# 96 more TensorE instructions ahead of the second recurrence layer's projection: a hybrid RWKV / attention / state-space kernel on one Trainium2 core

## What is computed

```python
for i in range(4):
    kind, j = i % 3, i // 3
    hx = rms_norm(x, norm_g[i]) * (1 + scale_x) + shift_x
    hc = rms_norm(ctx, norm_g[i]) * (1 + scale_c) + shift_c
    if kind == 0:    # h = [hc, hx]
        xs = h + (centred_shift(h) - h) * mu[:, None]        # six mixes
        r, k, v, g = xs[:4] @ w_rkvg
        # decay, iclr from xs[4], xs[5] by low-rank products
        for t in scan order, both directions, per head:       # 16 heads of 64
            sa = state @ kk[t]
            state = state * w[t] - sa (kk[t] * a[t])^T + v[t] k[t]^T
            y[t] = state @ r[t]
        out = (group_norm(y) + bonus) * silu(g) @ w_out
    x = x + gate * out
```

## Time and profile before

| | us |
|---|---|
| median of 3 runs | 7097.44 |
| lowest, highest | 7081.59, 7100.32 |
| profiled execution, its own time | 7083.38 |
| its span | 7081.5 |
| TensorE busy | 5788.8 (82%) |
| VectorE, ScalarE, GpSimd busy | 2986.5, 2066.1, 1883.9 |

### The profile page before, as it was taken

The page is one execution under the profiler, slowest core; times in us unless marked ns, Lnnn a source line. Parts: engine busy times, 40 slices in busy tenths (PEclk is TensorE's granted clock), DMA queues, the critical chain, the costliest instruction groups (busy, mean ns, idle before and its releaser), DMA issues. The chain is left out here.

```text
span 7081.5 us, 214110 instructions
## 1 busy us (share of the span) xinstructions
PE 5788.8 (82%) x92672; PEld 3901.0 (55%) x92672; DVE 2986.5 (42%) x6387; ACT 2066.1 (29%) x3451; POOL 1883.9 (27%) x2006
## 2 busy tenths in 40 slices
PE   5999788888878999788988759899966776767667
PEld 4555677777744554455445445445455555555553
DVE  7100566666632331555245772130134444544442
ACT  3000444455522221334123331110033333333330
POOL 3551344444413350000063300000033323333321
PEclk8999899999989999888989879999988888898888
DMA  3222110100022221311223462211200000000002
GB/s 124 96 96 75 38 37 29 37 29 29 29 80 109 96 78 41 94 48 48 84 95 105 86 105 92 92 61 67 74 23 31 31 24 30 14 31 31 31 24 86
DMA packets 192948, 430.53 MB, mean 61 GB/s; under 512 B 24384, under 2 KB 108224, under 8 KB 192192
## 3 DMA queue, kind: packets, MB, share of 16 engines
q1 hardware_dynamic: 157440, 322.85, 15.3%
q10 hardware_dynamic: 34752, 96.51, 3.4%
HBM read 313.41 MB, written 105.87 MB: 59 GB/s over the span
## 5 line engine op out<-in xcount | busy, mean ns | idle before, releaser
L382 PE MATMUL ps<-arena 128*128 128x512 f32 x4544 | 1686.7, 533 | 60.0 <-ACT arena L336 18.4
L382 PEld LDWEIGHTS ps<-arena 128*128 128x128 f32 x4544 | 863.1, 190 | 878.9 <-issue 811.1
L1887 PE MATMUL ps<-arena 64*64 64x64 f32 x35840 | 792.7, 233 | 428.1 <-issue 330.0
L1887 PEld LDWEIGHTS ps<-arena 64*64 64x64 f32 x35840 | 684.7, 145 | 474.5 <-issue 462.0
L158 POOL TENSOR_TENSOR arena<-arena 128x512 f32<-128x512 f32 (+1 forms) x360 | 337.2, 953 | 1704.0 <-DMA arena<-w_mod 1693.8
L2292 ACT COPY arena<-ps 128x512 f32<-128x512 f32 (+1 forms) x880 | 538.5, 627 | 804.7 <-PE ps L1887 796.5
L2437 POOL TENSOR_TENSOR arena<-arena 128x256 f32<-128x256 f32 (+1 forms) x320 | 316.8, 994 | 1288.5 <-DVE arena L2678 737.0
L540 PE MATMUL ps<-arena 128*128 128x512 f32 (+1 forms) x1152 | 423.0, 527 | 18.2 <-ACT arena L336 18.2
L2554 DVE TENSOR_TENSOR arena<-ps,arena 128x512 f32<-128x512 f32 x486 | 322.3, 687 | 175.5 <-PE ps L1874 124.0
L161 POOL TENSOR_TENSOR arena<-arena 128x256 f32<-128x256 f32 (+2 forms) x504 | 377.7, 761 | 51.2 <-issue 0.2
L2362 POOL MEMSET arena<- 128x1280 f32 (+4 forms) x22 | 15.1, 739 | 1331.5 <-POOLq L88 1331.5
(11 more groups left out here) (267 smaller groups left out, 9889.4 us busy)
## 6 DMA issues: line engine op xcount, KB each, us to landing
arena<-proj SPq DMA_DIRECT2D x158, 640.0 KB, 5.2
proj<-arena ACTq DMA_DIRECT2D x80, 640.0 KB, 3.8
arena<-w_mod SPq DMA_DIRECT2D x96, 512.0 KB, 7.7
arena<-rw_w SPq DMA_DIRECT2D x68, 512.0 KB, 3.4
xres<-arena ACTq DMA_DIRECT2D x24, 640.0 KB, 6.0
arena<-na_w_in SPq DMA_DIRECT2D x24, 512.0 KB, 3.7
arena<-x SPq DMA_DIRECT2D x16, 640.0 KB, 6.3
arena<-xres SPq DMA_DIRECT2D x16, 640.0 KB, 6.4
```

Source lines behind the costliest of these rows:

```text
L382: last = nc.tensor.matmul(k.ps[:, 3 * u + n, 0:b - a], w[:, c * P:(c + 1) * P], src[:, c, a:b], start=(c == 0), stop=(c == KT - 1))
L1887: last = PE.matmul(part_of(out, dst, hh, g, d), part(l, src, hh, g, d), rhs, start=True, stop=True)
```

## The change

96 increments of the unused semaphore stand behind the norm's matmuls of layer 3's projection, ahead of its first loop; layer 0 gets none.

```diff
+PROJECT_FILL = (0, 96)
 
 
 def rwkv_project(nc, k, j, dd, hid, mod_layer):
...
         @block.tensor
         def _(pe):
             normal.tensor_part(pe)
+            for _ in range(PROJECT_FILL[j]):
+                hold(k, pe)
             for n in range(4):
                 if n:
                     pe.wait_ge(xs_ready, n)
```

## The result

The changed kernel takes 6586.8 us (median of 4 executions, 6576.29 to 6588.68), the one before 7089.51 us in the same comparison (4 executions, 7069.52 to 7100.32). The ratio is 0.9291, with a 95% interval of 0.9266 to 0.9316. The prediction was 6590 us.

What follows compares the result with a forecast made beforehand. It took delivery of TensorE's instructions to bound layer 3's recurrence, TensorE's own work layer 0's. 7083.4 + 0 + 0 - 500 = 6583, given as 6590 us between profiled execution and median; range 6560 to 6625.

Steps and rivals of the forecast that it cites:

- The 96 increments at no cost: Ahead of layer 3's projection loop, under a 22.48 us wait for VectorE: 0 us, at most 0.4 us each, 16 past cover.
- The projection's four loops at no cost: Layer 3's projection: loops of 133 to 197 records stay buffered in either place; 0 us taken, at most 6 to win.
- The recurrence's loop, -500 us: Layer 3's inner loop moves to touch seven blocks, so its outer loop falls from 1724.0 to layer 0's 1224.0 us.
- the signs named for it: Layer 3: outer loop 1224 us within 15, about 109 instruction packets, none in passes 2 to 5 (77 us), clock 1.00.
- Blocks begin at 193 + 256 n: TensorE's instruction stream: dry points in both layers' recurrence loops placed the starts of 256-record blocks at 193 modulo 256.
- Seven stay, eight do not: Recurrence's inner loop of 1,685 records: stays in TensorE's instruction buffer touching 7 blocks (begin at place 0 to 107), not 8.
- Rival (a): Layer 3's inner loop still reloads each pass wherever it begins; 7023 us, or 7083 if the place brings nothing; chance 0.04.
- Rival (b): Layer 3's inner loop: seven blocks stay but each back edge costs a 3.79 us fetch, 121 us given back, 6711; chance 0.02.
- Rival (c): Ahead of layer 3's projection: increments dear, at 0.5 us each, and the loop still reloads; 7109 us; chance 0.01.

Runs made afterwards that it cites:

- the kernel with 33 records: 157 increments ahead of layer 3's projection in place of the changed kernel's 96, its inner loop ending 33 records into the eighth block; 6852.2 us.
- layer 0 with its 95 records in the eighth block: Against the changed kernel, the 96 increments stand in layer 0's projection in place of layer 3's; 7145.73 us.

## Why the prediction was right, point by point

**The 96 increments at no cost: right.** 96 x 0.150 = 14.4 us under a wait of 22.49. The upper bound of 0.4 us each was too high by a factor of 2.7, so the 16 us kept for it in the range were not needed. (A slip beside it: 96 increments of 0.45 us would pass the cover by 20.7 us, not by over 21.)

**The projection's four loops at no cost: right.** Their stretch takes 499.20 us as before, and undoing their move alone changes nothing that one execution tells.

**The recurrence's loop, -500 us: right in mechanism and size, one part of it misread.** The window of the loop gives -494, and the signs named for it came: 1230 us, 111 packets of q8, no packet in passes 2 to 5 and a clock of 1.00 in them. In the turn that I had cut, the parts came out as 57.5 us for passes 2 to 5 (57.6 predicted), 7.9 for a first pass (7.4) and 2.5 for the steps (0.7). Multiplied by turns they give 8 x 57.5 + 7 x 7.9 + 8 x 2.5 = 535, more than there was. This turn is not the mean one on either side: 134.3 + 49.2 + 35.7 = 219.2 us in the earlier trace rows, eight times that is 1754, and the loop took 1724; in the changed kernel 151.3, eight times that is 1210, and the loop took 1230. With all turns cut at the end of each pass's last matmuls (L2056, now L2061), passes 2 to 5 of the eight turns went from 1084.40 to 615.70 us, 468.7 less where the prediction's part was 461, and the seven stretches of steps and next first pass from 560.96 to 534.85, 26.1 less where its parts were 7 x (7.4 + 0.7) = 57. So the warm passes are nearly all of the gain, and the first passes were put too high. Some 4 us of the 7.4 (and as much of the 7.9) come from how the windows were cut: the one of layer 3 ends at 5452.70, and its pass's last matmuls end at 5449.45, so that it takes in most of the stand at the back edge behind the pass,

```profile
5452.88 0.34 PE L1887 MATMUL ps<-arena 64*64 64x64 f32 x7 [3.44 <-issue]
```

which belongs to the second pass; the one of layer 0 ends at 963.10, 0.9 us before its pass's last matmuls do. Cut at these ends the two first passes take 32.44 and 29.27 us, 3.2 apart. The total was safe from it because the prediction took the whole loop.

**"Blocks begin at 193 + 256 n": off by one record.** The step that failed is the reading of dry points from MATMUL rows alone. A matmul's weight load stands ahead of it as a record of its own, and at a dry point the load may be through while the matmul is not. The weight loads of the kernel before at that back edge say so (PEld in order of time; its MATMUL row has 7):

```profile
5233.70 0.24 PEld L1887 LDWEIGHTS ps<-arena 64*64 64x64 f32 x8 [4.00 <-issue]
```

Eight loads and seven matmuls are 15 records behind 16049 + 2, which gives 16066 = 194 + 62 x 256. Two of the other three dry points say the same (20 loads against 19 matmuls at L1874, 10 against 9 in layer 0's L1902; at L1928 both are 22). This cost nothing here, since the change had 27 places to spare (28 by the corrected count), but it made two expectations wrong by 470 to 500 us.

**"Seven stay, eight do not": too strict at the top.** What decides in these runs is how many records lie in the eighth block: 1 stays, 33 loses every second pass, 65, 95, 132, 147 and 148 lose all (the last is the kernel with 16 increments, which also has only one record in its first block). All these loops are equally long, so that the same series can be told by the records in the first block; no run here parts the two. Nine packets per lost pass fit one account: by then delivery has asked for a ninth block, and if the buffer holds eight, that evicts the loop's first. In the kernel with 33 records a cold pass has its eighth block only late, so that the ninth is not yet asked for at the branch, and the pass behind it is warm. The counts and the times of the packets are shown and fit; what the buffer holds and drops is argued only.

**Rival (a), a reload wherever the loop begins: refuted.** Five places of layer 3's loop (0, 79, 106, 107 and 108), and 79 in three ways (96 increments ahead of the projection, 96 behind it, 1,120 ahead), give 318 to 322 packets and no lost pass. The sentence of the Trainium skill ("Runtime: NRT & Kernel Launch", section "Instruction fetch mechanics") by which the instruction memory is two cache lines, and a branch out of them must fetch, does not hold for TensorE here: a branch back over 1,685 records lands with no gap. The 128 KiB in blocks of 16 KiB that the same section gives agree with what was measured, as far as that goes: packets of 16.4 KB, seven blocks that stay, and an eighth that may be touched by one record.

**Rival (b), a fetch at each back edge: refuted** by the pair of rows at 5241.82 and 5243.69 above.

**Rival (c), slower: refuted** in both of its conditions. Its price, over 0.45 us for an increment, is three times the measured one, and the loop no longer reloads.

## What to carry to other kernels

Where the same code runs at two places of a program, cut both out of the trace and compare; a difference with the same work, a full "issue" column and more packets on the instruction queue is code delivery, and the packets per pass say how many passes are lost. A loop whose body nearly fills the buffer should begin early in a block, and the numbers to compute are its first and last record modulo 256, with blocks placed by dry points read from weight loads and matmuls together. Moving it was free here because the filler lay under a wait, and any later edit ahead of the loop moves it again, so its place must be recomputed after each.

## What was unexpected in the hardware

One record decides 449 us: 7059.15 us with 16 increments, 6610.33 with 17. The buffer forgives a loop that touches an eighth block by one record and not one that has 65 there, with alternating passes of 19 and 32 to 35 us between them. A lost pass costs 14.6 us in the kernel before (468.7 / 32) and 16.4 in layer 0 with its 95 records in the eighth block ((1141.22 - 615.57) / 32), and the granted clock is lower in it: 0.90 in the one shown against 1.00 in a warm one. In the one turn compared, code without any branch back over turns was delivered no faster to its first pass (28.70 us) than code behind a branch (28.40). In the changed kernel what the branch between turns cost stayed hidden under a wait for VectorE of 4 to 5 us, and with the outer loop begun four records ahead of a block's end (17 increments) the stand was 5.89 to 7.37 us. And an increment of a semaphore that nobody waits for occupies TensorE's sequencer for 0.150 us.
